# Turning the last activated group of an expert inside its next down tile, behind three products

## The reference, cut to what matters

```python
def moe_swiglu(h, router, wg, wu, wd):            # first block: 8 experts, d_ff 2816, top 2
    ...
    for e in range(N_EXPERTS):
        out = out + dense_gate[:, e:e + 1] * swiglu(ht, wg[e], wu[e], wd[e])

def hierarchical_moe(h, w_rg, b_rg, w_re, b_re, w_gate, w_up, w_down):   # second: 4 groups of 4, d 256
    ...
    a = jnp.einsum('td,edf->tef', ht, w_gate)
    u = jnp.einsum('td,edf->tef', ht, w_up)
    hid = jax.nn.silu(a) * u * combine[..., None].astype(ht.dtype)
    out = jnp.einsum('tef,efd->td', hid, w_down)
```

## Time and profile before

| what | us |
|---|---|
| median of 3 runs (lowest 1775.97) | 1776.07 |
| the profiled execution | 1776.7 |
| its span, from first to last instruction | 1775.0 |
| TensorE busy in the span | 1671.7 |
| VectorE busy | 1285.5 |
| ScalarE busy | 1008.4 |
| mean granted TensorE clock, as a share of full speed | 0.965 |

### The profile page before, as it was taken

The page is one execution under the profiler, slowest core; times in us unless marked ns, Lnnn a source line. Parts: engine busy times, 40 slices in busy tenths (PEclk is TensorE's granted clock), DMA queues, the critical chain, the costliest instruction groups (busy, mean ns, idle before and its releaser), DMA issues.

```text
span 1775.0 us, 23849 instructions
## 1 busy us (share of the span) xinstructions
PE 1671.7 (94%) x9475; PEld 1357.1 (76%) x9475; DVE 1285.5 (72%) x1152; ACT 1008.4 (57%) x861; POOL 23.1 (1%) x37
## 2 busy tenths in 40 slices
PE   6989999897999999999999999999789999799997
PEld 6969999896777776767777676777588798788875
DVE  5984444796687888888787888888657545577764
ACT  4744334464476767767676767767444353266653
POOL 3000000000000000000000000000000000000000
PEclk9999999998899999999999999999979799799999
DMA  9535555433497989899798989989744334368860
GB/s 285 188 121 177 188 184 188 149 102 119 177 372 290 366 314 357 304 351 386 284 379 306 360 298 355 373 299 369 257 141 127 124 120 143 107 230 286 286 241 25
DMA packets 240762, 431.54 MB, mean 243 GB/s; under 512 B 11540, under 2 KB 121648, under 8 KB 240688
## 3 DMA queue, kind: packets, MB, share of 16 engines
q1 hardware_dynamic: 239200, 426.17, 68.8%
q10 hardware_dynamic: 1488, 4.34, 0.7%
HBM read 429.44 MB, written 1.05 MB: 243 GB/s over the span
## 4 chain that ended last, share of the span: by engine, by line
PE 75%; issue 14%; DVE 7%; ACT 3%; DMA 1%; POOL 0%; DVEq 0%; SPq 0%; POOLq 0%; ACTq 0%
PE PS L1033 22%; PE PS L1035 22%; PE PS L1034 22%; PE PS L1113 2%; DVE w_low L1524 2%; PE PS L1247 2%; PE PS L1279 1%; ACT w_high L804 1%; DVE hT_low L1524 1%; PE PS L1408 1%; ACT w_high L668 1%; PE PS L1407 1%; DVE h L1548 1%; DMA ring<-in_w_in_dram 1%; PE PS L1206 0%
## 5 line engine op out<-in xcount | busy, mean ns | idle before, releaser
L1524 DVE TENSOR_TENSOR w_low<-ring,w_high 128x2048 fp32r<-128x2048 f32 x402 | 917.4, 2289 | 321.0 <-ACT w_high L668 172.1
L804 ACT ACTIVATE w_high<-ring 128x2048 fp32r<-128x2048 f32 x306 | 585.5, 1918 | 270.6 <-PE PS L1035 270.4
L1033 PE MATMUL PS<-w_high,hT_high 128*96 128x512 f32 (+3 forms) x1184 | 421.0, 356 | 12.3 <-DVE hT_low L1524 7.3
L1035 PE MATMUL PS<-w_high,hT_low 128*96 128x512 f32 (+3 forms) x1184 | 413.4, 349 | 0.0
L1034 PE MATMUL PS<-w_low,hT_high 128*96 128x512 f32 (+3 forms) x1184 | 412.0, 348 | 0.0
L668 ACT ACTIVATE w_high<-ring 128x2048 fp32r<-128x2048 f32 x96 | 182.9, 1910 | 143.3 <-PE PS L1035 139.5
L1033 PE MATMUL PS<-hT_high,w_high 128*128 128x256 f32 x832 | 242.1, 291 | 8.2 <-DVE hT_low L1524 6.4
L1033 PEld LDWEIGHTS PS<-w_high,hT_high 128*96 128x96 f32 (+1 forms) x1184 | 196.6, 166 | 63.8 <-DVE hT_low L1524 8.0
L1034 PE MATMUL PS<-hT_low,w_high 128*128 128x256 f32 x832 | 239.1, 287 | 0.0
L1035 PE MATMUL PS<-hT_high,w_low 128*128 128x256 f32 x832 | 238.9, 287 | 0.0
L1033 PE MATMUL PS<-w_high,yT_high 128*96 128x512 f32 (+1 forms) x568 | 228.0, 401 | 8.2 <-DVE yT_low L1524 8.2
(11 more groups left out here) (289 smaller groups left out, 1306.7 us busy)
## 6 DMA issues: line engine op xcount, KB each, us to landing
ring<-in_moe_wg_dram SPq DMA_DIRECT2D x88, 1024.0 KB, 6.6
ring<-in_moe_wu_dram SPq DMA_DIRECT2D x88, 1024.0 KB, 7.0
ring<-in_moe_wd_dram SPq DMA_DIRECT2D x80, 1024.0 KB, 6.3
ring<-in_w_in_dram SPq DMA_DIRECT2D x36, 1024.0 KB, 5.6
ring<-in_w_gate_dram SPq DMA_DIRECT2D x16, 1024.0 KB, 6.4
ring<-in_w_up_dram SPq DMA_DIRECT2D x16, 1024.0 KB, 6.1
ring<-in_w_down_dram SPq DMA_DIRECT2D x16, 1024.0 KB, 5.9
ring<-in_ffn_wg_dram SPq DMA_DIRECT2D x11, 1024.0 KB, 5.4
```

The source lines that it names most:

```text
L804: act.activation(w_high[:, (s.base + k) % SPLITS, :], slot(w), ACT.Copy).then_inc(s.high_taken, 1)
L1033: mm(o, left_high, right_high, start=first, stop=False, skip_group_check=shared)
L1035: return mm(o, left_low, right_high, start=False, stop=last_one, skip_group_check=shared)
L1524: return tt(out_, whole, part.bitcast(F32), ALU.subtract)
```

## The change

`moe_tile` takes a function `between` and calls it in a down tile after the first call of `three()`, that is after three products of 512 columns into PSUM bank 4. In a turn that is not the last, the transposes of the last group (with their wait on `hid_ready`) are no longer issued between the gather and the first down tile, but from within that tile. In `moe2` they thereby also come behind `gather_weights`, which stands ahead of the tile. The last turn of each loop is as it was. No instruction is added or taken away.

```diff
-            def moe_tile(e, s, i, k):
+            def moe_tile(e, s, i, k, between=None):
...
+                            if between and c == 0 and hf == 0:
+                                between()
...
-                    moe_tile(e, s, i, k)
+                    inside = k == e.turn_at[-1] + 1 and not last
+                    moe_tile(e, s, i, k, (lambda: turn_hidden(e, s, i, e.groups - 1)) if inside else None)
...
                     if k == e.turn_at[-1] and not last:
                         pe.wait_ge(s.picked, i * 2 + (s.n["picked"] + 4))
                         for b in range(2):
                             gather_half(e, s, b)
-                        turn_hidden(e, s, i, e.groups - 1)
```

## The result

The changed kernel takes 1765.24 us in the median of 7 runs (1761.73 to 1769.24), the kernel before 1777.72 in 7 runs (one of them the outlier of 5672 us). The ratio is 0.9933, 95% interval 0.9915 to 0.9951, that is 8.7 to 15.1 us less. The forecast was 7.7 us less and a time of 1768.4. The profiled execution took 1764.35 us, its span is 1762.6 instead of 1775.0.

The account below looks back on a forecast made before the run. The prediction took TensorE to bound the kernel, busy 1671.7 of 1775.0 us. It summed 4.8 us in moe1 and 2.9 in moe2 to 7.7, so 1776.07 - 7.7 = 1768.4 us, with a range of 1764.5 to 1773.5.

Parts of the forecast that it names:

- The bound and the ceiling: Whole kernel: TensorE bounds it, reordering returns only its idle time; waits at the transposes cap the gain at 16.1 us.
- Three products ahead of the wait, `moe1`, 4.8 us: At 7 moe1 turn ends, three products of 0.23 us fill 0.69 us of a 0.92 us idle hole: 4.8 us.
- `moe2`, 2.9 us: At 3 moe2 turn ends, weight gather and three products fill 0.98 us of a 1.37 us hole: 2.9 us.
- Nothing for splitting the tile: Transposes inside the down tile's sum cost 0, at worst 0.06 us, which falls in the hole.
- Waits moved ahead, the turned group later, the queues: Turn ends: down tile's waits cost 0, turned group keeps 3.4 us of cover, loads have 4.2 us of slack.
- the stop at the third tile: TensorE's 0.41 us wait at 571.43 on VectorE's low half, behind the turn's end; claimed to move along without growing.
- handed on: Rival: TensorE waits the saved time at its next stop, giving 1776.1 us, or about 1772 for one loop; chance 0.12.
- The clock did not fall: Rival denied here: the clock drops behind the turn-end holes of both loops, giving 1775 to 1782 us; chance 0.03.
- the hole closes altogether: Rival: all TensorE idle time at the turn-end transposes goes, 10.6 or 12.5 us, giving 1765.5 or 1763.6; chance 0.05.
- the likeliest case of 1767 to 1770: Whole kernel: the forecast of 7.7 us less, give or take 1.5, around 1768.4 us; chance 0.80.
- price for a fall of the clock: Last moe2 turn, behind 2.40 us of idle: 9 products at clock 0.50 cost 0.7 us extra, or 1.4.
- The sum: Both loops together: 4.8 + 2.9 = 7.7 us less, 1768.4 us, 0.43% faster.

Follow-up runs that it names:

- e4: Kernel before, with ScalarE's silu and VectorE's product of the last group moved ahead of the same step's weight pass; TensorE's order unchanged: 1754.37 us, ratio 0.9877.
- e8: The change together with the early activated rows of e4: 1759.32 us, ratio 0.9900.
- e7: The change, but with the transposes behind all twelve products of the first down tile instead of three: 1762.54 us, ratio 0.9927.
- e3: The change, but with the transposes behind six products of the down tile instead of three: 1761.77 us, ratio 0.9920.
- e9: The kernel before itself, unedited, for a second trace: 1777.21 us, ratio 0.9998.
- e5: The changed kernel itself, unedited, for a second trace and more runs: 1764.05 us, ratio 0.9928.
- e1: The change in the moe1 loop only, moe2 as in the kernel before: 1766.42 us, ratio 0.9951.
- e2: The change in the moe2 loop only, moe1 as in the kernel before: 1771.0 us, ratio 0.9970.
- e11: Kernel before plus four 128x1024 VectorE padding copies (2.9 us) between the moe1 loop and the following norms: 1774.15 us, ratio 0.9992.
- e10: Kernel before plus two 128x1024 VectorE padding copies (1.5 us) between the moe1 loop and the following norms: 1774.85 us, ratio 0.9990.
- e6: The change plus four 128x1024 VectorE padding copies (2.9 us) between the moe1 loop and the following norms: 1766.88 us, ratio 0.9955.
- e12: The change plus two 128x1024 VectorE padding copies (1.5 us) between the moe1 loop and the following norms: 1769.59 us, ratio 0.9960.

## Why the prediction was right or wrong

- **The bound and the ceiling.** Right for the loops, where only TensorE's idle time changed. "Idle time of TensorE and nothing else" did not hold for the whole span: TensorE's busy time fell by 6.4 us (1671.7 to 1665.3), 5.3 of them in the untouched attention stretch.
- **Three products ahead of the wait, `moe1`, 4.8 us.** Right, in the mechanism and in size. The transposes start 1.19 us behind the gather before and after, a turn went from 102.5 to 101.8, the wait from 6.4 to 1.6 us in 7. e4 shows that the arrival was set by the weight passes, as read from the earlier trace rows.
- **`moe2`, 2.9 us.** Right, 3 x 1.04 = 3.1.
- **Nothing for splitting the tile.** Right: with the wait gone the split tile is neither faster nor slower (e8 against e4, 101.4 us a turn of `moe1` each, 42.50 and 42.48 of `moe2`).
- **Waits moved ahead, the turned group later, the queues.** Right. ScalarE's idle time ahead of its next conversion went from 2.44 to 1.75 us, by the 0.69 that was forecast. Even behind twelve products (e7) the group comes in time. No new wait appears on a landing, and the stop at the third tile is 0.41 us before and after, and the sum of TensorE's waits for the low half of a weight tile is unchanged, before and after:

```profile
PE PS L1033 <- DVE w_low L1524: 4.5, 11, 0.6
```

```profile
PE PS L1033 <- DVE w_low L1526: 4.5, 11, 0.6
```

- **Rivals.** The hole did not close; it takes six products (e3). The gain was not handed on. The clock did not fall in the turns that the change touches (1.00 in the rows above). The time alone would have misled: 1765.24 is next to the 1765.5 of "the hole closes altogether" and under the likeliest case of 1767 to 1770, while the trace shows the hole still open by 0.2 us in `moe1` and 0.34 in `moe2`. Its price for a fall of the clock, 0.7 to 1.4 us behind a hole of 2.40, has about the right size, but the fall is not certain: in e3 the clock stays at 1.00 behind the same hole of 2.40 us (58.7 us from the last gather to the last scatter), in e7 it doesn't (60.2 us at 0.97).
- **The sum, and the step that failed.** "The forecast (7.7 us, give or take 1.5 for what the modelled ends hide)" took the loops' gain as the whole effect. The term for what lies outside the loops was 0 and measured 3 to 6 us in the traces and about 5 in the medians: 12.5 less 7.9 = 4.6 in the first set, 1777.21 - 1764.05 = 13.2 less 7.9 = 5.3 in e9 and e5. I asked of the clock only whether it could fall behind the holes, and not how far stretches whose mean clock was 0.91 and 0.95 vary by themselves. The time of 1765.24 stayed in the range because that reached down to 1764.5 for another rival, the closing hole, which didn't happen: that part was luck.
- **That the extra comes from the clock** is shown as far as the traces and the runs' clocks go: same instructions, unequal times, the clock unequal the same way, and 8.6 us of difference left at equal clock. Why the change has the higher mean clock stays open. That the change itself raises it, and would in another kernel, is not shown.

## What to carry to other kernels

Price a reordering by the start-to-start distance of what fills the hole, and look at what sets the arrival that ends the hole: taking the unneeded weight pass out of the way (e4, 14.9 us by the turns) was worth more than filling the hole (7.9), and made the filling worthless. In a kernel with stretches below full clock, the median can move by as much again as a small edit saves (e1: 4.8 us by its turns, 10.5 by its median). Judge such an edit by the length of its own turns in the trace, compare runs of equal granted clock, and credit it with a surplus in the median only after controls such as padded kernels.

## What the runs showed of the hardware that was not expected

The attention stretch, the same some 1510 instructions of TensorE each time, took 229.3 (e2), 230.0 (the change), 230.9 (e1, e4, e11), 231.9 (e10), 232.0 (e6), 232.3 (e5), 232.6 (e3, e9), 235.5 (e8) and 235.6 us (before, e7, e12), at mean granted clocks of 0.93 down to 0.91. `moe2` in its old form took 195.7 (e1, e11), 195.8 (e10), 197.4 (before) and 200.4 us (e9) at 0.96, 0.96, 0.95 and 0.93. The Trainium skill has a statement near this: the page "TensorE: Matmul & The Clock Gate", section "Part 1: The HAM clock gate (the "warmup" mystery)", says that the number of slow products with which a kernel starts varies from run to run of one kernel. It calls that penalty under 1% of a typical span. The swings here lie in the middle of the kernel as well; 6 us are 0.35% of its span, within that bound, but nearly as large as the effect that was to be measured. Apart from that, a 128x1024 float32 copy from SBUF to SBUF took 0.69 us on VectorE, while line 1548 of the kernel before, which multiplies tiles of that size by a column and by a second tile, takes 2.48 us for two instructions.
